# A token tile's first head ranked ahead of the second tile's work

## The reference, cut to what matters

```python
x = x + mod_x[2] * merge_branches(o_ax, o_bx, zx[4], w_branch_a, w_branch_b, w_out)
x = x + mod_x[5] * peer_ffn(modulate(rmsnorm(x, norm2_g), mod_x[3], mod_x[4]), ...)

def one_chunk(xc):                       # 128 tokens
    q = (xc @ peer_wq).reshape(128, 8, 2, 128)
    s = einsum('chpd,hpkd->chpk', q, peer_keys)
    sv, si = top_k(s, 16)
    cand = sv[..., 0, :, None] + sv[..., 1, None, :]       # 16 x 16 pairs
    top_s, pos = top_k(cand, 16)
    eidx = the experts' numbers at pos
    gate = softmax(top_s)
    act = gelu(einsum('chkd,cd->chk', peer_u[eidx], xc))
    return einsum('chk,chkd->cd', gate * act, peer_v[eidx])
```

## Time and profile before

| | |
|---|---|
| median of 3 runs | 2663.58 us (2661.52 to 2667.41) |
| the profiled execution | 2661.96 us |
| its span | 2660.1 us |
| PE busy | 2437.5 us, 92% |
| DVE busy | 1549.4 us, 58% |
| ACT busy | 554.1 us, 21% |
| POOL busy | 663.1 us, 25% |
| indirect DMAs of the whole program | 277.51 MB |

### The profile page before, as it was taken

The page is one execution under the profiler, slowest core; times in us unless marked ns, Lnnn a source line. Parts: engine busy times, 40 slices in busy tenths (PEclk is TensorE's granted clock), DMA queues, the critical chain, the costliest instruction groups (busy, mean ns, idle before and its releaser), DMA issues.

```text
span 2660.1 us, 45997 instructions
## 1 busy us (share of the span) xinstructions
PE 2437.5 (92%) x18972; PEld 1698.6 (64%) x18972; DVE 1549.4 (58%) x3156; ACT 554.1 (21%) x1277; POOL 663.1 (25%) x512
## 2 busy tenths in 40 slices
PE   8999999999999998998999888899998977887887
PEld 6588696476887943754678778888865533332333
DVE  1873376537734754576457445455038776777765
ACT  1252000014330000015333333231011111111111
POOL 0000014300000241000013657440004455444552
PEclk9999999999999998999999999999999999888999
DMA  4332344443233446314452101003349999999997
GB/s 186 154 127 101 153 159 158 165 160 153 96 127 142 175 158 267 129 63 190 144 173 64 34 18 34 19 34 131 141 162 379 420 422 421 421 422 421 421 421 311
DMA packets 91239, 523.84 MB, mean 197 GB/s; under 512 B 39729, under 2 KB 39729, under 8 KB 43441
## 3 DMA queue, kind: packets, MB, share of 16 engines
q0 software_dynamic: 39360, 277.51, 25.6%
q1 hardware_dynamic: 51696, 243.80, 24.6%
HBM read 511.85 MB, written 9.44 MB: 196 GB/s over the span
## 4 chain that ended last, share of the span: by engine, by line
PE 66%; DVE 13%; DMA 10%; issue 5%; POOL 2%; ACT 2%; DVEq 2%; POOLq 1%; ACTq 0%; SPq 0%
PE psum L557 33%; PE psum L1858 23%; DMA mem<-weights,mem 10%; PE psum L2339 5%; DVE mem L3243 4%; DVE mem L2695 3%; PE psum L799 2%; PE psum L573 1%; PE psum L2311 1%; POOL mem L3293 1%; DVE mem L3042 1%; POOL mem L3393 1%; PE psum L1868 1%; POOLq L3350 1%; DVEq L2880 0%
## 5 line engine op out<-in xcount | busy, mean ns | idle before, releaser
L1858 PE MATMUL psum<-mem 64*64 64x64 f32 (+6 forms) x12340 | 880.6, 268 | 60.2 <-DVEq L3046 15.5
L557 PE MATMUL psum<-mem 128*128 128x128 f32 (+9 forms) x4856 | 909.4, 358 | 13.9 <-DVE mem L1172 3.5
L1858 PEld LDWEIGHTS psum<-mem 64*64 64x64 f32 (+3 forms) x12340 | 707.1, 150 | 232.9 <-issue 129.7
L557 PEld LDWEIGHTS psum<-mem 128*128 128x128 f32 (+4 forms) x4856 | 684.2, 183 | 231.4 <-issue 154.2
L2339 PE MATMUL psum<-mem 128*128 128x512 f32 x1024 | 500.8, 647 | 119.7 <-ACT mem L2659 119.7
L2339 PEld LDWEIGHTS psum<-mem 128*128 128x128 f32 x1024 | 207.2, 207 | 406.7 <-issue 243.7
L3393 POOL DMA_INDIRECT mem<-weights,mem x256 | 315.5, 1232 | 524.4 <-PE psum L2339 264.5
L3243 DVE CUSTOM_DVE_ANT_0 mem<-mem 128x1024 f32<-128x1024 f32 x256 | 307.4, 1224 | 138.5 <-DMA mem<-weights,mem 132.0
L2695 DVE TENSOR_TENSOR mem<-psum,mem 128x512 f32<-128x512 f32 (+2 forms) x180 | 111.5, 630 | 255.9 <-PE psum L1858 226.6
L3293 POOL TENSOR_TENSOR mem<-mem 128x512 f32<-128x512 f32 (+3 forms) x148 | 205.7, 1402 | 153.7 <-DVEq L3011 119.3
L1522 POOL TENSOR_TENSOR mem<-mem 128x1024 f32<-128x1024 f32 x14 | 27.1, 1934 | 782.4 <-ACTq L1073 782.4
(11 more groups left out here) (282 smaller groups left out, 1530.6 us busy)
## 6 DMA issues: line engine op xcount, KB each, us to landing
mem<-weights SPq DMA_DIRECT2D x100, 2048.0 KB, 7.4
rates_dram<-mem POOLq DMA_DIRECT2D x16, 512.0 KB, 4.7
mem<-rates_dram SPq DMA_DIRECT2D x32, 256.0 KB, 4.5
mem<-weights SPq DMA_DIRECT2D x7, 1024.0 KB, 6.8
mem<-weights SPq DMA_DIRECT2D x2, 2176.0 KB, 7.8
mem<-weights,mem POOLq DMA_INDIRECT x256, 26.4
mem<-weights SPq DMA_DIRECT2D x2, 1536.0 KB, 7.9
mem<-weights SPq DMA_DIRECT2D x2, 1152.0 KB, 8.4
```

The costliest lines, as they stand in the source:

```text
L557: ins = pe.matmul(out, lhsT, rhs, start=start, stop=stop, skip_group_check=skip)
L1858: ins = pe.matmul(out, lhsT, rhs, start=start, stop=stop, skip_group_check=skip)
```

## The change

The new order begins with head 0 of tile 0. PE makes the output products (0,0), (0,1) and five eighths of (1,0), transposes tile 0, ends (1,0), makes chunks 0 and 1 of tile 0's queries, a quarter of (1,1), head 0's scores, the rest of (1,1), chunks 2 and 3, h2's transposes, head 1's scores; then the queries of wq1 for tile 0, tile 1's transposes, wq1 for tile 1. The queries of wq0 for tile 1 come behind the sums of groups 0 and 1, and its scores behind group 2. DVE ranks head 0 between its adds of (1,0) and (1,1), head 1 after tile 1's norm. ACT evacuates tile 1's transposes as well. keysT is loaded ahead of wq1. The ranking pieces of unit 2 move from groups 0, 1, 2 to 1, 2, 3. The sums that stand between the queries are three groups further on.

Two of the buffers lie in the slot that wq2 will fill. In the new order they are used once before it: as the sixth and seventh buffer (`BEFORE_QUERY = [5, 6]`, numbers of gathers), once wq0's last queries have begun; SP loads wq2 when row 6 is summed. So ten gathers have a fresh buffer, then eight buffers turn over three times (n = 10 to 33), ten twice (n = 34 to 53), and then all 16.

```diff
-    free_at_once = [base, base + 2560] + [ptop[0] + 2 * D * i for i in range(4)]
+    free_at_once = [base + 2560] + [ptop[0] + 2 * D * i for i in range(4)]
+    behind_norm = base
...
-    first_bufs = [*range(8)] * 3 + [8, 9, *range(8)] * 2
+    first_bufs = [*range(5), 8, 9, 5, 6, 7] + [*range(8)] * 3 + [8, 9, *range(8)] * 2
+    BEFORE_QUERY = [5, 6]
...
-            if name == "wq2":
+            if name == "wq1":
 
                 sp.wait_ge(*obx_ready.at(0))
                 sp.wait_ge(*merged2_ready.at(0))
                 sp.dma_start(keysT, ...)
 
+            if name == "wq2":
+                sp.wait_ge(*rows_summed.at(0, BEFORE_QUERY[-1]))
             sp.wait_ge(weights.used, used0 + n + 2)
...
+        for half in range(2):
+            out_products(dve_ring.open(pe, "out2"), 0, half)
+        late_out = dve_ring.open(pe, "out2")
+        out_products(late_out, 1, 0, 0, 5)
+        tile_transposes(0)
+        out_products(late_out, 1, 0, 5, 8)
...
+        pe.wait_ge(*hT2_by_act.at(0, 2))
+        tile_queries(wq0, 0, (0, 1))
+        late_out = dve_ring.open(pe, "out2")
+        out_products(late_out, 1, 1, 0, 2)
         pe.wait_ge(lora_landed, 48)
         pe.wait_ge(*qTp_ready.at(0, 0))
-        score_products(scored, 0, 0)
-        first_queries(b, 1, (2, 3)).then_inc(act_ring.full, 1)
+        score_products(0, 0, (0, 1))
+        out_products(late_out, 1, 1, 2, 8)
+        item_now["fresh"] = True
+        tile_queries(wq0, 0, (2, 3))
         h2_transposes(0)
+        pe.wait_ge(*qTp_ready.at(0, 1))
+        score_products(0, 0, (2, 3))
+        wq1 = km_view(item("wq1"), 512)
+        item_now["fresh"] = False
+        tile_queries(wq1, 0)
+        tile_transposes(1)
+        pe.wait_ge(*hT2_by_act.at(0, 3))
+        tile_queries(wq1, 1)
+        key_scores(1)
+        sums([0, 1])
+        tile_queries(wq0, 1)
+        sums([2])
         key_scores(0, (1,))
         h2_transposes(1)
-        queries(1)
-        key_scores(1)
+        pe.drain().then_inc(weights.used, 1)
         for c in range(4):
-            sums([c])
+            sums([3 + c])
             query_chunk(2, c)
-        sums([4])
+        sums([7])
         key_scores(2)
         for c in range(4):
-            sums([5 + c])
+            sums([8 + c])
             query_chunk(3, c)
-        sums([9])
+        sums([12])
         key_scores(3)
...
+        add_out(0, 0)
+        add_out(0, 1)
+        tile_norm(0)
+        add_out(1, 0)
+        choose_first(0)
+        add_out(1, 1)
+        tile_norm(1)
+        choose_first(1)
         expert_gates(0)
         expert_gates(1)
...
-                if b % 8 == 0:
+                phase = b % 8 - (ahead == 2)
+                if phase == 0:
                     rank(ahead)
...
+            if m is None and at == behind_norm:
+                pool.wait_ge(*hT2_by_act.at(0, 3))
+            for g, done in ((1, 3), (3, 6)):
                 if m is None and at == behind_query[g][0]:
-                    pool.wait_ge(*qTp_ready.at(0, g + 1))
+                    pool.wait_ge(*qTp_ready.at(0, done))
+            if n == BEFORE_QUERY[0]:
+                pool.wait_ge(weights.used, used0 + SLOTS + ITEM2["wq0"] + 1)
+            elif m == BEFORE_QUERY[0]:
+                pool.wait_ge(*qTp_ready.at(0, 5))
```

More of the change, by code:

```diff
@@ L2301, in tile_transposes, with out_products @@
             for q in range(2):
[L2302 to L2313, removed]
-                last.then_inc(dve_ring.full, 1)
-        item_now["fresh"] = False
-        def queries(g):
-            channel_major(act_ring, "qp", hT, km_view(item(f"wq{g}"), 512), 8, 4)
+                transposes(act_ring, "hT", [xn[:, t, (4 * q + c) * P:(4 * q + c + 1) * P] for c in range(4)])
+        out_weights = [km_view(item(f"out{half}"), 512) for half in range(2)]
+        def out_products(b, t, half, first=0, end=8):
+            for k in range(first, end):
+                last = pe.matmul(b, mg2[:, k, t * P:(t + 1) * P], out_weights[half][:, k, :], start=k == 0, stop=k == 7)
+                if k == 0 and t == half:
+                    last.then_inc(weights.used, 1)
+            if end == 8:
+                last.then_inc(dve_ring.full, 1)
+        for half in range(2):
[4 more added lines that the diff above has]
+        out_products(late_out, 1, 0, 5, 8)
         def query_chunk(g, c):
@@ L2357, in first_queries @@
                     last = mm(b[:, c * P:(c + 1) * P], w[:, k, c * P:(c + 1) * P], hT[:, k, t * P:(t + 1) * P], k == 0, k == 7)
-            return last
+            last.then_inc(act_ring.full, 1)
         def h2_transposes(t):
@@ L2605, in tile_root, with tile_evac, tile_queries @@
             A(csd2[:, t:t + 1], css2[:, t:t + 1], ACT.Sqrt, bias=C["eps"], scale=1.0 / D).then_inc(root2_ready.sem, 1)
[L2607 to L2614, removed]
-        tile_root(1)
-        def first_queries(t):
-            done(A(qTp[:, 0:4, t * P:(t + 1) * P], take("qp").rearrange("p (c n) -> p c n", c=4), ACT.Copy))
+        def tile_evac(t):
+            for q in range(2):
+                b = take("hT")
+                for c in range(4):
+                    k = 4 * q + c
+                    last = A(hT[:, k, t * P:(t + 1) * P], b[:, c * P:(c + 1) * P], ACT.Identity, bias=AB[:, 5, k:k + 1], scale=AB[:, 4, k:k + 1])
+                done(last)
+            act.drain().then_inc(hT2_by_act.sem, 1)
+        def tile_queries(g, t, first=0, end=4):
+            done(A(qTp[:, 4 * g + first:4 * g + end, t * P:(t + 1) * P],
+                   take("qp")[:, first * P:end * P].rearrange("p (c n) -> p c n", n=P), ACT.Copy))
             act.drain().then_inc(qTp_ready.sem, 1)
@@ L2625, in query_pair, with key_scores @@
                 act.drain().then_inc(qTp_ready.sem, 1)
-        def key_scores(g, tiles=range(TT)):
+        def key_scores(g, tiles=range(TT), first=0, end=4):
             for t in tiles:
-                done(A(sp_[:, t, 4 * g:4 * g + 4, :], take("sp").rearrange("p (c n) -> p c n", c=4), ACT.Copy))
+                done(A(sp_[:, t, 4 * g + first:4 * g + end, :],
+                       take("sp")[:, first * P:end * P].rearrange("p (c n) -> p c n", n=P), ACT.Copy))
                 act.drain().then_inc(scores_ready.sem, 1)
@@ L3137, in _ @@
             v.drain().then_inc(xn2_ready.sem, 1)
[L3138 to L3144 removed]
+        SCORED = {(0, 0): 0, (0, 1): 1, (0, 2): 2, (1, 2): 3, (1, 0): 4, (0, 4): 5, (1, 4): 6, (0, 6): 7, (1, 6): 8}
         def rank(u):
             t, h, n = UNITS[u]
[L3149 removed]
+            v.wait_ge(*scores_ready.at(0, SCORED[t, h]))
             lists = range(2 * h, 2 * h + 2 * n)
@@ L3260, in add_experts, with choose_first @@
                 tt(x[:, t, s], x[:, t, s], peer_out[half], ALU.add).then_inc(out_ready.sem, 1)
-        for u in range(2):
+        def choose_first(u):
             rank(u)
```

106 lines of the change are left out of this document (52 added, 54 removed).

## The result

The changed kernel takes 2672.1 us (median of 6 runs, 2669.27 to 2675.84) where the one before took 2662.59 beside it: a ratio of 1.0033, 95% interval 1.0021 to 1.0046. A second set of nine runs (e5) gave 1.0031 (1.0017 to 1.0045). It is slower, and outside the range of the forecast. The profiled execution took 2670.75 us, its span 2668.8.

The account below looks back on a forecast made before the run. The DMA queue of 256 gathers, 2.49 us each, bounds the kernel. Gather 23 comes 7.5 us ahead; less 2.9, 1.5 and 1.4 the lead is 1.7, taken as 1: 2662.6 from 2663.58, range 2655.5 to 2669.5.

Parts of the forecast that it names:

- The earlier start: Start of the gather stream: first gather issued at 1979.7 us, 14.0 earlier, and landed at 1985.3, 14.7 earlier.
- What hides the moved edits: Up to gather 10: moved loads and PE work are covered, and gather 10 lands without a gap at full clock.
- gap (a): Refill at gather 16, which needs row 8 summed behind wq0's tile 1 on PE: 0.9 us lost.
- Bytes that join the stream: Loads of wq2 and wq3, now among the gathers: 5.0 us each, 10.0 us that the gathers have to give.
- Refill gaps: Waits for a free buffer before gathers 16, 34, 56 and 59: 0.9, 2.9, 1.5 and 1.4 us.
- Gap (b): Gather 34 waits for the wq2 queries: 30.2 us after row 23 lands, against 27.3 for eleven gathers; 2.9 lost.
- Gap (c): Gather 56 waits for the wq3 queries: 53.7 us against 52.2 for 21 gathers; 1.5 lost.
- (b) to (d): Waits at gathers 34, 56 and 59, for wq2 queries, wq3 queries and last scores: 2.9, 1.5 and 1.4 us.
- PE's clock: PE idles 2.9 and 2.2 us near gathers 8 and 10; a clock drop costs 0 or twice 3.0 us.
- the rival: Slower, 2669.5 us, 17%: PE's clock falls in both idle stretches near gathers 8 and 10, a loss of 5 to 6.
- The faster rival: 2656 us, 24%: the gaps before gathers 34, 56 and 59 don't open, so the lead is 7.5 us.
- the start that doesn't move: 2673 us, 3%: DVE or the scores come no earlier, and the 10.0 us of loads remain.

Follow-up runs that it names:

- e5: The changed kernel again, with no edit, timed on the chip beside other follow-ups: 2670.8 us, ratio 1.0031 to the kernel before.
- e1: Changed kernel with ACT's copy of wq0's tile-1 queries moved behind the weights of group 2: 2666.01 us, ratio 1.0007.
- e8: As e6, with the loads of wq2 and wq3 cut to 64 of 4096 columns: 2656.74 us, ratio 0.9986.
- e3: Changed kernel with the loads of wq2 and wq3 cut to 64 of 4096 columns: 2666.25 us, ratio 1.0005.
- e6: As e1, with each wq2 and wq3 query chunk and the last scores one group of sums earlier on PE, ACT's order matching: 2661.1 us, ratio 0.9993.
- e13: As e7, with filler matmuls on PE, 4 ahead of sums 4 and 3 meant for sums 8: ratio 0.9976.
- e14: As e13, with the second tile's transposes ahead of the last chunk of wq1 for tile 0: ratio 0.9980.
- e7: As e6, with wq0's tile-1 queries cut in two halves, one ahead of sums 0, one between sums 1 and 2: 2656.65 us, ratio 0.9979.
- e9: Changed kernel with filler matmuls on PE, 8 ahead of sums 4 and 9 ahead of sums 8: ratio 1.0050.
- e12: Changed kernel with fewer filler matmuls on PE, 4 ahead of sums 4 and 4 ahead of sums 8: ratio 1.0032.

## Why the prediction was wrong

**The earlier start: right.** 39.1 for the issue and 5.7 us for the landing, to a tenth.

**What hides the moved edits: wrong. This is the step that failed first, and the largest single cause shown.** The forecast went through PE's and DVE's rows of the changed program and let ACT's copies pass as 0.6 us each. In gap (a) it put wq0's tile 1 ahead of row 8's sum on PE, but not ahead of the tanh on ACT. ACT worked through its program in the order written: its instruction of 0.6 us that waits for 7.3 us of PE held the tanh behind it. DVE stood still for 6.43 us there and PE for 1.88, and e1 shows the price: some 7 us by the ratios, out of 9.5 between the forecast and the median, and 3.7 to 4.4 by the profiles, out of 7.6 at gather 255. With this alone mended the kernel is at 1.0007 (0.9997 to 1.0018); the forecast of 2662.6 was a ratio of 0.9996, just below that interval. Gather 23 then lands at 116.0 where the forecast had 116.1, and gather 34 at 147.2 for 146.3; what is left lies between 34 and 59.

**Bytes that join the stream, 10.0: mis-sized as a price, though not a source of the miss.** e8 gives 0.5 for wq2 and 3.8 for wq3; e3 against e5 gives 0.0 and 4.9. Each load does hold the gathers up by its 5 us of bytes (4.9 and 5.3), but where the next turn is late anyway, the loss without the load would be as long: what is lost is the longer one, not the sum. The forecast weighed one against the other at gather 16, which is why (a) came to only 0.9, and so its gather 23 is nearly right (116.1 against 117.4 after, 116.0 in e1). As the price of the loads, 10.0 is twice too much.

**Refill gaps: right in place and in first size, short of what comes around them.** All four opened, behind the releasers named. Gather 16 cost 1.4 (forecast 0.9), 34 cost 1.7 (2.9), 56 cost 2.6 (1.5), 59 cost 0.9 (1.4): 6.6 against 6.7. That the two totals agree is luck, for the chains under them were longer than forecast. Two things had no term.

The gather behind a gap was late again: 17 by 1.4, 35 by 0.9, 57 by 1.1; in e1, 35 and 36 by 1.4 and 57 by 1.6.

Gathers 27 to 32 lost 3.9 in ordinary turns of eight buffers, in which the forecast let the queue run at its pace: gather 24 was issued at 2056.86, rel 113.5, behind sums 4 with its 3.81 us of waiting, and found two gathers ahead, the nearer due in 1.4 us (before, three to six ahead from 24 to 29).

So from 23 to 34 it was 32.7 us against 30.2, and from 34 to 59 68.7 against 65.0, with gather 59's successors at the pace before; these make 6.2 of the 7.6 us at gather 255, gather 23 another 1.3. Two terms of the chains were too short. Gap (b) let group 5's sums start 2.9 us after row 23 lands, as before; it was 5.1, because PE was still on sums 4, late and at a lower clock, and on a chunk of queries (3.4 where sums 4 ran at full clock, e1). This is 2.2 of the 2.5 us up to gather 34. Gap (c) was given 36.7 us from row 35 to the sums of group 11; it was 38.6. No run isolates those 1.9, but with the chunks one group earlier it is 36.7 again (e6).

```profile
2065.81 7.03 PE L2344 MATMUL psum<-mem 128*128 128x512 f32 x16
```

That is group 5; gather 23 landed at 2060.73. e6 shows the place of (b) to (d): with the chunks one group earlier gathers 34, 56 and 59 come at the pace, and 34 to 59 take 62.6.

**PE's clock: the rival had the right sign and named the wrong place.** It gave 2669.5 and a slower kernel at 17%. The clock did fall near gather 8: with 2.86 us of idling, 80 query instructions took 10.92 us, at a granted clock of 0.84, where e1 has 9.29.

```profile
1992.05 10.92 PE L1862 MATMUL psum<-mem 128*128 128x128 f32 x80 [2.86 <-ACTq L2632]
```

Gather 8, issued at 2002.02, still found two gathers ahead and landed 2.47 us behind gather 7, so the drop did not reach the queue there. e13 kept that idling and ran the same queries at full clock, so e14 against e13 doesn't test it. Where the clock did count is a place that the rival didn't name: at sums 4, 1.7 us between gathers 23 and 34 (5.1 against 3.4), behind an idle stretch that the late landing of gather 19 had made longer. The faster rival (gaps don't open) is refuted by the four landings; the start that doesn't move, by the first row. (The text's 17 and 3% for the slower cases add up to 0.20, its last line has 0.19.)

Of the range: it allowed each gap 1 or 2 us and took the chains as known. It had no room for a wait of the size of a PE stage, which is what a missed position in a queue costs.

## What to carry to other kernels

When an edit reorders one engine's work, walk every other engine's program past each moved item and ask what is queued behind it, however short the item is; here a copy of 0.6 us cost some 7 by the ratios. In a stream fed by few buffers, price the turn of a buffer stage by stage and take the longest of bytes and turns, not their sum. A slot that refills a dry queue costs its latency again, so an early start that is given back at the refills is worth nothing until the stages that release buffers are moved forward too (e6, e7).

## What the runs showed of the hardware

A group of sums takes 7.03 to 7.13 us at full clock (2.4 GHz). Behind idle time on PE it takes that, or mostly 8.83, or up to 10.16, by how much of it the lower level (1.2 GHz) covers: the granted clock was 1.00 in the changed kernel's group of 7.03 us, 0.81 in that of 8.83 and 0.70 in that of 10.14. The same place can do either: after 1.87 us of idling 7.13 in e9 and 8.83 in e12, after 3.27 us 10.14 in e7 and 8.83 in e13. Of the groups that stand alone in the 16 profiles between 1975 and 2250 us, 7 of 26 were slow behind 1.7 to 2.3 us of idling, 26 of 48 behind 2.3 to 3.2, and 34 of 35 behind 3.2 to 4.6. None of the 168 behind less idle time or none was slow.

Executions of one program spread over some 10 us (e5: 2665.7 to 2677.1; the kernel before, 32 runs: 2655.1 to 2666.4). In the profiles that is mostly the start of the first output product, so one profile can't rank kernels that are 0.2% apart; counted from that start, two profiles of the changed kernel agree within 0.7 us at gather 255, while e12's, with fillers and slow early groups, is 4 off.
